# Expert rows of a mixture of experts in 14 blocks instead of 16, with pieces of 32, 64 and 128 columns

## The chip, the cores and the metric

The kernel is one program on one NeuronCore of a Trainium2 chip. Its time is the device time of one execution in microseconds (us). All arithmetic is float32. The profile is of one execution, taken by the hardware profiler; engines are TensorE (PE for matmuls, PEld for its weight loads), VectorE (DVE), ScalarE (ACT), GpSimd (POOL) and SyncE (SP, which here only issues DMAs).

## What is computed

Two layers of a hybrid backbone over 640 tokens (128 context, 512 latent) of width 1024. Each layer has attention, a chunked MLP and a gated recurrence, and then a mixture of 16 experts, of which each token uses two. The change concerns the mixture alone:

```python
eidx = top-2 experts of each token, within its best group of four
dest = place of each (token, expert) row, experts padded to blocks
xb = xt[row_tok].reshape(n_blocks, MOE_BLOCK, D)

def expert_block(args):
    xblk, e = args
    a = jax.nn.silu(xblk @ wg[e]) * (xblk @ wu[e])   # 1024 -> 512, twice
    return a @ wd[e]                                  # 512 -> 1024
yb = lax.map(expert_block, (xb, block_e)).reshape(n_rows, D)
y = jax.ops.segment_sum(yb * row_w[:, None], row_tok, num_segments=T)
```

There are 1280 (token, expert) rows in each layer. An expert has three weight matrices (gate, up, down) of 2 MB each, so a layer reads 48 matrices, 100.7 MB.

## The kernel before

The program is written by hand for each engine; nothing is scheduled by a planner. In the expert stage of a layer the experts are sorted by how many rows they got, on the chip. The expert of rank s has a fixed capacity `CAPS[s]` and a fixed first row `BASES[s]`, and rows beyond a capacity go to overflow blocks, which are run in a loop of `OVB` passes that skip when there is nothing to do (in this execution all are skipped). The capacities sum to 2048 rows, 16 blocks of 128 rows (`NBK`). `RUN` lists the blocks in the order in which they run, with the rank of the first and of the last 64 rows of each: 12 blocks belong to one expert, 4 to two.

TensorE does for each block i, in this order: `hidden(i, 0)` (gate), `tokens_in(i + 1)` (8 transposes of the next block's tokens, L843), `hidden(i, 1)` (up), `outputs(i - 1)` (down of the block before, in two halves of 512 columns) and `turn_hidden(i)` (4 transposes, L866). All three products go through `product` (L855): over k (8 for gate and up, 4 for each half of down) it multiplies the block's 128 columns, which stand still in the array, with 512 columns of an expert's weights. In a block of two experts, two matmuls of 64 columns stand in place of one of 128, and write partitions 0 to 63 and 64 to 127 of the same bank. The program has one float32 matmul where the trace has two instructions.

Weights come through 8 slots of 2 MB (`moe_slots`). `moe_matrices` orders the matrices by the block that needs them first: the gates of a block's new experts, then their ups, then their downs. SP loads matrix m into slot m mod 8, once the last block that uses matrix m - 8 has read it (`moe_used`); `LAST` holds that block. GpSimd gathers a block's token rows from DRAM (L1287), VectorE copies the transposed tokens out (L1849), ScalarE applies silu (L1155) and copies the transposed hidden rows (L1163), VectorE and ScalarE copy a half of the output each (L1855, L1146), and ScalarE's queue stores the block to DRAM (L1151). When all blocks are stored, GpSimd gathers each token's two rows (L1311), ScalarE makes diagonal matrices of the routing weights (L1192), and TensorE combines them (L534, L535).

Of the kernel before, what the change touches and what calls it, by code (L numbers as in the profile page):

```python
# [28 lines left out]
P = 128  # L29
# [29 lines left out]
GB = 4  # L59
NE = 16  # L60
DFF = 512
OVB = 8

CAPS = [256, 256, 192, 192] + [128] * 6 + [64] * 6
BASES = [sum(CAPS[:i]) for i in range(NE)]
NBK = sum(CAPS) // P
NB = NBK + OVB

RUN = [(7, (4, 4)), (0, (0, 0)), (1, (0, 0)), (13, (10, 11)), (2, (1, 1)), (3, (1, 1)), (14, (12, 13)), (4, (2, 2)),
       (5, (2, 3)), (6, (3, 3)), (15, (14, 15)), (8, (5, 5)), (9, (6, 6)), (10, (7, 7)), (11, (8, 8)), (12, (9, 9))]
NSLOT = 8

def moe_matrices():

    order, last = [], {}
    for i, (_, who) in enumerate(RUN):  # L80
        new = [s for s in sorted(set(who)) if s not in last]
        order += [(s, j) for j in range(3) for s in new]
        for s in who:
            last[s] = i
    return order, last

MATS, LAST = moe_matrices()
# [29 lines left out]
def nth(l, per, n):  # L118
    return l * per + n
# [12 lines left out]
def build_program(nc, A):  # L132
    with ExitStack() as ctx:
# [6 lines left out]
        def dram(name, shape):  # L140
            return nc.dram_tensor(name, shape, F32, kind="Internal").ap()
# [5 lines left out]
        x_dram = dram("x_dram", [T, D])  # L147
        exp_dram = dram("exp_dram", [NB * P, D])

# [23 lines left out]
        def view(off, n, pattern=None, **kw):  # L173
            v = ar[:, off:off + n]
            return v.rearrange(pattern, **kw) if pattern else v
# [46 lines left out]
        yb = [view(26624 + 1024 * s, 1024) for s in range(2)]  # L222
# [6 lines left out]
        at_row = view(12288, 10 * P, "p (a r) -> p a r", a=10)  # L229
        at_block = view(12288 + 10 * P, 10 * NB, "p (a b) -> p a b", a=10)  # L230

# [21 lines left out]
        def sm(n):  # L253
            o[0] += n
            return small[:, o[0] - n:o[0]]
# [18 lines left out]
        mhalf = sm(20)  # L274
        spare = sm(OVB)
        modc = sm(4 * KD).rearrange("p (m y k) -> p m y k", m=2, y=2)
        posi = ismall[:, 0:10].rearrange("p (t k) -> p t k", t=NT)
        rowi, blki = ismall[:, 50:60], sb("blki", [P, 10], I32)[:]
        rowf, blkf = sm(10), sm(10)
        ids = ismall[:, 10:10 + NB]  # L280
        novi = ismall[:, 36:37]
        bexi = ismall[:, 40:40 + OVB]
        esi = ismall[:, 62:62 + NE]
# [2 lines left out]
        chosen = view(26624, 80)  # L286
        before = view(27584, 96)
        R9 = view(27680, OVB * NE, "p (j e) -> p j e", j=OVB)
        R9s = view(27808, OVB)
        ck, srt, es, cbs = [view(27816 + NE * i, NE) for i in range(4)]  # L290
        capb = view(27880, 2 * NE, "p (m e) -> p m e", m=2)
        above = view(27912, NE * NE, "p (e f) -> p e f", e=NE)
# [42 lines left out]
        xg_in = [sem("xg_in0"), sem("xg_in1")]  # L335
        xT_done, xT_evac = sem("xT_done"), sem("xT_evac")
        gate_done, up_done, sg_ready, a_ready = sem("gate_done"), sem("up_done"), sem("sg_ready"), sem("a_ready")
        aT_done, aT_ready, y_done = sem("aT_done"), sem("aT_ready"), sem("y_done")
        yA_evac, yB_evac = sem("yA_evac"), sem("yB_evac")
        y_stored = [sem("y_stored0"), sem("y_stored1")]  # L340
# [10 lines left out]
        def until(eng, signal, n):  # L351

            eng.wait_ge(signal, n)
            eng.sem_inc(passed[eng.engine], 1)
# [24 lines left out]
        def moe_used(l, m):  # L380

            s_, j = MATS[m]
            return (gate_done, up_done, y_done)[j], (32 if j == 2 else 16) * l + (LAST[s_] + 1) * (2 if j == 2 else 1)

        def s3(v, k=KD):
            return v.rearrange("p (k c) -> p k c", k=k)
# [21 lines left out]
        def _(sp):  # L408
# [5 lines left out]
            for l in range(DEPTH):  # L414
# [50 lines left out]
                for m in range(len(MATS) - 3, len(MATS)):  # L465
                    until(sp, *moe_used(l, m))
                nov = sp.value_load(novi[0:1, :], min_val=0, max_val=OVB)
                with sp.Fori(0, OVB) as j:
# [25 lines left out]
        def _(pe):  # L494
# [19 lines left out]
            for l in range(DEPTH):  # L514
# [103 lines left out]
                for ci, c in enumerate(JOBS):  # L618
# [21 lines left out]
                    for j in range(NL + 1):  # L640
# [11 lines left out]
                        for w in range(NT):  # L652
                            tk = slice(w * P, (w + 1) * P)
                            for h in range(2):
                                r = slice(64 * h, 64 * h + 64)
# [19 lines left out]
                    if dr == 1:  # L675
# [12 lines left out]
                        for w in range(NT):  # L688
                            ent = (0 if w == 0 else 1 + w, 1 if w == 0 else 2 + w)
                            for d_ in range(2):  # L690
                                for h in range(2):
                                    r = slice(64 * h, 64 * h + 64)
# [114 lines left out]
                for t in range(NT):  # L807
                    pe.wait_ge(tr_evac, nth(l, N_TR, 2 * NT + 2 * t + 2))
                    for half in range(2):
# [3 lines left out]
                        w = s3(slotA(SLOT_OF[7 + half]))  # L813
# [14 lines left out]
                for a in range(2 * NT):  # L828
                    mm = pe.matmul(bank(5)[:, 0:NB], at_row[:, a, :], at_block[:, a, :],
                                   start=a == 0, stop=a == 2 * NT - 1)  # L830
# [3 lines left out]
                def tokens_in(i):  # L834

                    p = i % 2
                    pe.wait_ge(xg_in[p], l * 128 + 16 * (i // 2 + 1))
                    if i:
                        pe.wait_ge(xT_evac, nth(l, NBK, i))
                    if i >= 2:  # L840
                        pe.wait_ge(aT_ready, nth(l, NBK, i - 1))
                    for k in range(KD):
                        mm = pe.transpose(psum[:, 3072 + k * P:3072 + (k + 1) * P], xg[p][:, k * P:(k + 1) * P], ident)  # L843
                    mm.then_inc(xT_done, 1)

                def product(out, act_T, i, j, kn, cs):

                    a, b = RUN[i][1]
                    parts = [(a, slice(0, P))] if a == b else [(a, slice(0, 64)), (b, slice(64, P))]
                    for s_, r in parts:  # L850
                        pe.wait_ge(*moe_landed(l, MAT[s_, j]))
                    for k in range(kn):
                        for s_, r in parts:
                            w = s3(moe_slots[MAT[s_, j] % NSLOT], kn)
                            mm = pe.matmul(out[r, :], act_T[:, k, r], w[:, k, cs], start=k == 0, stop=k == kn - 1)  # L855
                    return mm
# [4 lines left out]
                def turn_hidden(i):  # L861
                    pe.wait_ge(a_ready, nth(l, NBK, i + 1))
                    if i + 1 < NBK:
                        pe.wait_ge(xT_evac, nth(l, NBK, i + 2))
                    for q in range(4):
# [64 lines left out]
        def _(act):  # L930
# [18 lines left out]
            for l in range(DEPTH):  # L949
# [45 lines left out]
                for b, dst, fn in ((1, kf, ACT.Sigmoid), (2, qf, ACT.Copy)):  # L995
# [4 lines left out]
                    for c in (range(5) if b == 1 else (0, 4)):  # L1000
                        pb = unit_ready(AT[b, c])
                        if c < 4:
                            a = act.activation(dst[:, c, P:T], pb, fn)
                        else:
                            a = act.activation(dst[:, :, 0:P], pb.rearrange("p (c t) -> p c t", c=4), fn)
# [20 lines left out]
                for ci, c in enumerate(JOBS):  # L1026
                    at = {second: n for n, first, second in UNITS[ci]}
# [9 lines left out]
                    for j in range(NL):  # L1037
# [4 lines left out]
                        if j == 1:  # L1042
# [4 lines left out]
                            a, b = (kfac, qfac) if c < 2 else (qfac, kfac)  # L1047
# [94 lines left out]
                def y_half(i):  # L1142
                    act.wait_ge(y_done, nth(l, 2 * NBK, 2 * i + 2))
                    if i >= 2:
                        act.wait_ge(y_stored[i % 2], l * 128 + 16 * (i // 2))
                    act.activation(yb[i % 2][:, W:D], bank(5), ACT.Copy).then_inc(yB_evac, 1)  # L1146

                def y_store(i):
                    act.wait_ge(yA_evac, nth(l, NBK, i + 1))
                    act.wait_ge(yB_evac, nth(l, NBK, i + 1))  # L1150
                    act.dma_start(exp_dram[RUN[i][0] * P:(RUN[i][0] + 1) * P, :], yb[i % 2]).then_inc(y_stored[i % 2], 16)  # L1151

                for i in range(NBK):
                    act.wait_ge(gate_done, nth(l, NBK, i + 1))
# [11 lines left out]
                y_half(NBK - 1)  # L1166
                y_store(NBK - 1)

                until(act, y_stored[0], l * 128 + 128)
                until(act, pos_ready, l + 1)  # L1170
                nov = act.value_load(novi[0:1, :], min_val=0, max_val=OVB)
                with act.Fori(0, OVB) as j:
# [17 lines left out]
                for t in range(NT):  # L1190
                    for q in range(2):
                        a = act.activation(by_weight[:, 2 * t + q, :], ident, ACT.Copy, scale=wt[:, t, q:q + 1])  # L1192
# [8 lines left out]
        def _(gp):  # L1201
            gp.memset(condW[:], 0.0).then_inc(cond_zero, 1)
            gp.memset(mhalf, -0.5)
            for s_ in range(NE):
                gp.memset(table[:, 0, s_:s_ + 1], float(CAPS[s_]))
                gp.memset(table[:, 1, s_:s_ + 1], float(BASES[s_]))
            gp.memset(zeros, 0.0)
# [6 lines left out]
            for l in range(DEPTH):  # L1214
# [66 lines left out]
                until(gp, h_stored[0], l * 48 + 48)  # L1281
                until(gp, h_stored[1], l * 32 + 32)
                until(gp, ids_ready, l + 1)
                for i, (blk, _) in enumerate(RUN):
                    if i >= 2:
                        until(gp, xT_done, nth(l, NBK, i - 1))
                    gp.indirect_dma_start(xg[i % 2], None, tok_dram,  # L1287
                                          bass.IndirectOffsetOnAxis(ap=ids[:, blk:blk + 1], axis=0)).then_inc(xg_in[i % 2], 16)
                until(gp, pos_ready, l + 1)
                until(gp, xT_done, nth(l, NBK, NBK))  # L1290
                nov = gp.value_load(novi[0:1, :], min_val=0, max_val=OVB)
# [10 lines left out]
                        gp.dma_start(spare[0:1, bass.ds(j, 1)], bass.AP(A["router_bias"].tensor, 0, [[1, 1], [1, 1]])).then_inc(ov_g, 16)  # L1302
                until(gp, ov_g, l * (16 * OVB) + 16 * OVB)

                until(gp, y_stored[0], l * 128 + 128)
                until(gp, y_stored[1], l * 128 + 128)
                until(gp, ov_st, l * (16 * OVB) + nov * 16 + 16)

                for t in range(NT):
# [15 lines left out]
        def _(v):  # L1325
# [64 lines left out]
            for l in range(DEPTH):  # L1390
# [355 lines left out]
                for t in range(NT):  # L1746
                    dr_()
                    a = tt(before[:, (t + 1) * NE:(t + 2) * NE], before[:, t * NE:(t + 1) * NE], M[:, t, :], ALU.add)
# [52 lines left out]
                for q, oh in enumerate((oh1, oh2)):  # L1801
# [12 lines left out]
                dr_()  # L1814
                tt(at_block, blkf.unsqueeze(2).to_broadcast([P, 2 * NT, NB]),
                   cst[:, C_IOTA:C_IOTA + NB].unsqueeze(1).to_broadcast([P, 2 * NT, NB]), ALU.is_equal)
                tt(at_row, rowf.unsqueeze(2).to_broadcast([P, 2 * NT, P]),
# [33 lines left out]
                def y_half(i):  # L1851
                    v.wait_ge(y_done, nth(l, 2 * NBK, 2 * i + 1))
                    if i >= 2:
                        v.wait_ge(y_stored[i % 2], l * 128 + 16 * (i // 2))
                    v.tensor_copy(yb[i % 2][:, 0:W], bank(4)).then_inc(yA_evac, 1)  # L1855

                tokens_out(0)
# [121 lines left out]
```

## Time and profile before

| | |
|---|---|
| median of 3 runs | 2076.75 us (2075.97 to 2078.27) |
| the profiled execution, its own time | 2085.36 us |
| its span, first to last instruction | 2083.5 us |
| mean granted TensorE clock | 0.936 of 2.4 GHz |
| expert stage, layer 0 / layer 1 | 372.0 / 368.7 us |
| TensorE busy in them | 362.2 / 359.7 us |

The expert stage is taken from the first gate matmul to the end of the last output matmul. In a row of the timeline the first number is the start in us from the span's start and the second the time from the first start to the last end of the instructions that the row merges (xN). Matmuls overlap with the next, so a product's cost is read from its start to the next row's start. What follows in brackets is idle time before the row, and what ended it.

### The profile page before, as it was taken

The page shows a single profiled execution, that of the slowest core. Times are in us where ns is not written, and L with a number is a line of the kernel's source. Part 1 is how long each engine was busy: PE and PEld are TensorE (multiplying, and loading weights), DVE is VectorE, ACT ScalarE, POOL GpSimd, SP SyncE. Part 2 cuts the span into 40 slices and gives each one's busy share as a digit, 9 for nine tenths or more (in the row PEclk, how much of TensorE's full clock was granted, in tenths as well). Part 3 has the DMA queues.
Part 4 walks back from the last instruction along what each step waited for, and adds up shares of the span by engine and source line. Part 5 has one row for each costly group of instructions (what it writes and reads, how often), then busy time and mean ns, then how long its engine had stood idle before and what let it go on. Part 6 is the DMA issues. An engine that isn't in the chain of part 4 may idle for free. (4 is left out here: it accounts for less than half of the span.)

```text
span 2083.5 us, 20602 instructions
## 1 busy us (share of the span) xinstructions
PE 1809.4 (87%) x7528; PEld 927.7 (45%) x7528; DVE 755.3 (36%) x1179; ACT 374.4 (18%) x695; POOL 310.7 (15%) x348
## 2 busy tenths in 40 slices
PE   3999999788956999999799999988798399999983
PEld 1464555554443443434345445554545243443431
DVE  0036567374462110111060575746636310110105
ACT  1323122243010000000141422213411000000002
POOL 0001266000000000000130223630000000000005
PEclk9999999899977999999899999998998599999996
DMA  9421111565019687799603012136121696797934
GB/s 364 151 98 41 36 54 46 207 238 194 21 51 364 251 328 291 286 358 379 220 38 125 13 46 84 47 132 222 54 75 42 249 348 233 294 357 299 393 124 151
DMA packets 142086, 380.43 MB, mean 183 GB/s; under 512 B 9732, under 2 KB 15876, under 8 KB 135332
## 3 DMA queue, kind: packets, MB, share of 16 engines
q1 hardware_dynamic: 111840, 292.31, 37.5%
q10 hardware_dynamic: 21108, 55.36, 7.5%
q0 software_dynamic: 9040, 31.46, 4.1%
q8 instruction: 61, 1.00, 0.2%
q14 instruction: 37, 0.30, 0.0%
HBM read 343.65 MB, written 35.45 MB: 182 GB/s over the span
## 5 line engine op out<-in xcount | busy, mean ns | idle before, releaser
L855 PE MATMUL psum<-sb_arena 128*128 128x512 f32 (+1 forms) x1248 | 494.1, 596 | 10.6 <-DMA sb_arena<-w_up 9.1
L583 PE MATMUL psum<-sb_wA,sb_arena 128*128 128x512 f32 x800 | 365.3, 605 | 0.9 <-DMA sb_wA<-w_in 0.9
L855 PEld LDWEIGHTS psum<-sb_arena 128*128 128x128 f32 (+1 forms) x1248 | 192.5, 171 | 269.7 <-issue 257.7
L855 PE MATMUL psum<-sb_wA,sb_arena 128*128 128x512 f32 (+1 forms) x672 | 278.4, 611 | 9.3 <-DMA sb_wA<-w_up 6.6
L583 PEld LDWEIGHTS psum<-sb_wA,sb_arena 128*128 128x128 f32 x800 | 147.5, 192 | 165.3 <-issue 158.0
L1329 DVE TENSOR_TENSOR sb_arena<-sb_arena 128x320 f32<-128x320 f32 (+8 forms) x252 | 170.8, 719 | 13.4 <-POOL sb_arena L1264 3.8
L1849 DVE COPY sb_arena<-psum 128x1024 f32<-128x1024 f32 x32 | 39.2, 1225 | 344.3 <-PE psum L843 344.3
L855 PEld LDWEIGHTS psum<-sb_wA,sb_arena 128*128 128x128 f32 (+1 forms) x672 | 103.3, 170 | 120.2 <-issue 109.7
L1495 DVE COPY_PREDICATED sb_arena<-sb_masks,psum 128x640 f32<-128x640 uint8 x128 | 112.4, 878 | 90.8 <-PE psum L656 71.5
L574 PE MATMUL psum<-sb_arena,sb_wA 128*128 128x128 f32 (+1 forms) x512 | 140.4, 435 | 0.0
L815 PE MATMUL psum<-sb_wA,sb_arena 128*128 128x512 f32 x320 | 140.3, 599 | 0.0
L1287 POOL DMA_INDIRECT sb_arena<-tok_dram,sb_ismall x32 | 30.3, 946 | 654.1 <-PE psum L843 539.6
L1329 DVE TENSOR_TENSOR sb_arena<-sb_arena,psum 128x512 f32<-128x512 f32 x38 | 26.1, 687 | 272.3 <-PE psum L855 227.7
L1264 POOL TENSOR_TENSOR sb_arena<-sb_arena 128x640 f32<-128x640 f32 x56 | 80.7, 1444 | 287.4 <-ACT sb_arena L1039 251.5
L656 PEld LDWEIGHTS psum<-sb_arena 64*128 64x128 f32 x1280 | 79.4, 193 | 62.8 <-issue 56.1
L656 PE MATMUL psum<-sb_arena 64*128 64x128 f32 x1280 | 91.6, 287 | 14.9 <-DVE sb_arena L1495 12.7
L574 PEld LDWEIGHTS psum<-sb_arena,sb_wA 128*128 128x128 f32 x512 | 77.0, 191 | 60.0 <-issue 59.3
L1146 ACT ACTIVATE sb_arena<-psum 128x512 f32<-128x512 f32 x32 | 19.1, 597 | 461.4 <-PE psum L855 461.4
L1217 POOL TENSOR_TENSOR sb_small<-sb_small 128x4 f32<-128x4 f32 (+3 forms) x24 | 27.5, 1146 | 448.3 <-DVEq L1615 220.1
L815 PEld LDWEIGHTS psum<-sb_wA,sb_arena 128*128 128x128 f32 x320 | 60.9, 192 | 74.8 <-issue 74.8
L1329 DVE TENSOR_TENSOR sb_arena<-psum,sb_gate_mod 128x512 f32<-128x512 f32 (+1 forms) x30 | 26.1, 870 | 133.6 <-PE psum L815 87.8
L1155 ACT ACTIVATE sb_arena<-psum 128x512 f32<-128x512 f32 x32 | 19.2, 599 | 284.2 <-PE psum L855 284.2
(184 smaller groups left out, 1685.1 us busy)
## 6 DMA issues: line engine op xcount, KB each, us to landing
sb_arena<-w_gate SPq DMA_DIRECT2D x22, 2048.0 KB, 18.5
sb_arena<-w_down SPq DMA_DIRECT2D x22, 2048.0 KB, 15.8
sb_wA<-w_up SPq DMA_DIRECT2D x16, 2048.0 KB, 19.4
sb_arena<-w_up SPq DMA_DIRECT2D x16, 2048.0 KB, 15.5
sb_wA<-w_ada SPq DMA_DIRECT2D x13, 2048.0 KB, 7.7
sb_wA<-w_in SPq DMA_DIRECT2D x12, 2048.0 KB, 9.6
sb_arena<-w_ada SPq DMA_DIRECT2D x11, 2048.0 KB, 7.6
sb_wA<-w_gate SPq DMA_DIRECT2D x10, 2048.0 KB, 18.0
```

Of the source, the lines that this page charges most:

```text
L574: mm = pe.matmul(out, w[:, k, cc_ * P:(cc_ + 1) * P], hT[:, k, tok], start=k == 0, stop=k == KD - 1)
L583: mm = pe.matmul(unit_bank(n), hT[:, k, t * P:(t + 1) * P], w[:, k, :], start=k == 0, stop=k == KD - 1)
L656: mm = pe.matmul(U(h)[:, tk], ks[r, tk], qs[r, tk], start=True, stop=True)
L815: mm = pe.matmul(bank(n % 3), hT[:, k, t * P:(t + 1) * P], w[:, k, :], start=k == 0, stop=k == KD - 1)
L855: mm = pe.matmul(out[r, :], act_T[:, k, r], w[:, k, cs], start=k == 0, stop=k == kn - 1)
L1155: act.activation(sg[i % 2], bank(2 * (i % 2)), ACT.Silu).then_inc(sg_ready, 1)
L1217: gp.tensor_tensor(dst, src, mhalf[:, 0:dst.shape[1]], ALU.pow).then_inc(rstd_ready, 1)
L1264: gp.tensor_tensor(Kb[:, j % 2], kf[:, c], Eb[:, (j - 1) % 2], ALU.mult).then_inc(K_ready, 1)
L1287: gp.indirect_dma_start(xg[i % 2], None, tok_dram, bass.IndirectOffsetOnAxis(ap=ids[:, blk:blk + 1], axis=0)).then_inc(xg_in[i % 2], 16)
L1329: return v.tensor_tensor(out, a, b, op)
L1495: v.copy_predicated(w5(ATT[:, dr, h, :]), mk, w5(psum[:, (3 + 2 * h) * 512:(3 + 2 * h) * 512 + T])).then_inc(lv_acc, 1)
L1849: v.tensor_copy(xgT[i % 2], psum[:, 3072:4096].rearrange("p (k t) -> p k t", k=KD)).then_inc(xT_evac, 1)
```

## The change

The capacities are now in steps of 32 rows: 256, 224, 192, 192, 128, four of 96, six of 64, and 32. They sum to 1792, 14 blocks. `ROWS` puts the ranks in a row one behind the other, so that an expert's rows may start in the middle of a block and cross into the next; `block_parts` cuts each block's share into pieces of 128, 64 or 32 rows. Blocks run in the order of their rows. By `block_parts` they are (rank: columns):

| block | pieces | new matrices |
|---|---|---|
| 0 | 8: 64, 8: 32, 15: 32 | 6 |
| 1 | 4: 128 | 3 |
| 2 | 5: 64, 5: 32, 14: 32 | 6 |
| 3 | 14: 32, 6: 32, 6: 64 | 3 |
| 4, 5 | 0: 128 | 3, 0 |
| 6 | 7: 64, 7: 32, 11: 32 | 6 |
| 7 | 11: 32, 1: 32, 1: 64 | 3 |
| 8 | 1: 128 | 0 |
| 9 | 12: 64, 3: 64 | 6 |
| 10 | 3: 128 | 0 |
| 11 | 9: 64, 2: 64 | 6 |
| 12 | 2: 128 | 0 |
| 13 | 10: 64, 13: 64 | 6 |

`OVB` goes from 8 to 10, so that 24 block rows exist as before. The other lines of the diff follow the new count in semaphore values (`PAIR` is the number of even and odd blocks).

```diff
-OVB = 8
+OVB = 10
-CAPS = [256, 256, 192, 192] + [128] * 6 + [64] * 6
-BASES = [sum(CAPS[:i]) for i in range(NE)]
+CAPS = [256, 224, 192, 192, 128] + [96] * 4 + [64] * 6 + [32]
+ROWS = (8, 15, 4, 5, 14, 6, 0, 7, 11, 1, 12, 3, 9, 2, 10, 13)
+BASES = [sum(CAPS[r] for r in ROWS[:ROWS.index(s)]) for s in range(NE)]
 NBK = sum(CAPS) // P
+PAIR = [(NBK + 1) // 2, NBK // 2]
 NB = NBK + OVB
-RUN = [(7, (4, 4)), (0, (0, 0)), (1, (0, 0)), (13, (10, 11)), (2, (1, 1)), (3, (1, 1)), (14, (12, 13)), (4, (2, 2)),
-       (5, (2, 3)), (6, (3, 3)), (15, (14, 15)), (8, (5, 5)), (9, (6, 6)), (10, (7, 7)), (11, (8, 8)), (12, (9, 9))]
+def block_parts(i):
+    parts = []
+    for s in ROWS:
+        at, end = max(BASES[s], i * P) - i * P, min(BASES[s] + CAPS[s], i * P + P) - i * P
+        while at < end:
+            w = next(w for w in (P, 64, 32) if at % w == 0 and at + w <= end)
+            parts.append((s, slice(at, at + w)))
+            at += w
+    return parts
+RUN = [block_parts(i) for i in range(NBK)]
...
                 def product(out, act_T, i, j, kn, cs):
-                    a, b = RUN[i][1]
-                    parts = [(a, slice(0, P))] if a == b else [(a, slice(0, 64)), (b, slice(64, P))]
-                    for s_, r in parts:
+                    for s_ in sorted({s_ for s_, _ in RUN[i]}):
                         pe.wait_ge(*moe_landed(l, MAT[s_, j]))
                     for k in range(kn):
-                        for s_, r in parts:
+                        for s_, r in RUN[i]:
                             w = s3(moe_slots[MAT[s_, j] % NSLOT], kn)
                             mm = pe.matmul(out[r, :], act_T[:, k, r], w[:, k, cs], start=k == 0, stop=k == kn - 1)
...
                 def y_store(i):
-                    act.dma_start(exp_dram[RUN[i][0] * P:(RUN[i][0] + 1) * P, :], yb[i % 2]).then_inc(y_stored[i % 2], 16)
+                    act.dma_start(exp_dram[i * P:(i + 1) * P, :], yb[i % 2]).then_inc(y_stored[i % 2], 16)
...
-                for i, (blk, _) in enumerate(RUN):
+                for i in range(NBK):
                     gp.indirect_dma_start(xg[i % 2], None, tok_dram,
-                                          bass.IndirectOffsetOnAxis(ap=ids[:, blk:blk + 1], axis=0)).then_inc(xg_in[i % 2], 16)
+                                          bass.IndirectOffsetOnAxis(ap=ids[:, i:i + 1], axis=0)).then_inc(xg_in[i % 2], 16)
```

How TensorE's instructions stand, at two places. The first is the start of the expert stage in layer 0. `sb_wA` and `sb_arena` hold the weight slots, `psum` the results; the size is that of the output, columns of the block by 512. Before, block 0: tokens, gate, next tokens, up, hidden transposes, gate of block 1.

```order
L843 MATMUL psum<-sb_cst,sb_arena 128x128 x8
L855 MATMUL psum<-sb_wA,sb_arena 128x512 x8
L843 MATMUL psum<-sb_cst,sb_arena 128x128 x8
L855 MATMUL psum<-sb_wA,sb_arena 128x512 x8
L866 MATMUL psum<-sb_cst,sb_arena 128x128 x4
L855 MATMUL psum<-sb_arena 128x512 x8
```

After, the last two k of block 0's gate (six more like them stand ahead), the next block's tokens, and the first k of its up. In the gate the 64 and the first 32 columns are of rank 8 and the last 32 of rank 15.

```order
L869 MATMUL psum<-sb_wA,sb_arena 64x512
L869 MATMUL psum<-sb_wA,sb_arena 32x512 x2
L869 MATMUL psum<-sb_wA,sb_arena 64x512
L869 MATMUL psum<-sb_wA,sb_arena 32x512 x2
L859 MATMUL psum<-sb_cst,sb_arena 128x128 x8
L869 MATMUL psum<-sb_wA,sb_arena 64x512
L869 MATMUL psum<-sb_wA,sb_arena 32x512
L869 MATMUL psum<-sb_arena 32x512
```

Where one row of 8 whole-width matmuls stood, there are now 24 matmuls in two widths that take turns at each k. The second place is a block of several experts in the middle of the stage, between the hidden transposes and the next tokens. Before, block 3 (64 + 64), where all rows of a product have one width:

```order
L855 MATMUL psum<-sb_arena 128x512 x16
L866 MATMUL psum<-sb_cst,sb_arena 128x128 x4
L855 MATMUL psum<-sb_arena 64x512 x16
L843 MATMUL psum<-sb_cst,sb_arena 128x128 x8
L855 MATMUL psum<-sb_wA,sb_arena 64x512 x16
L855 MATMUL psum<-sb_arena 128x512 x8
```

After, block 3 (32 + 32 + 64): the hidden transposes of block 2 and the first two k of the gate.

```order
L869 MATMUL psum<-sb_wA,sb_arena 128x512 x8
L880 MATMUL psum<-sb_cst,sb_arena 128x128 x4
L869 MATMUL psum<-sb_wA,sb_arena 32x512
L869 MATMUL psum<-sb_arena 32x512
L869 MATMUL psum<-sb_arena 64x512
L869 MATMUL psum<-sb_wA,sb_arena 32x512
L869 MATMUL psum<-sb_arena 32x512
L869 MATMUL psum<-sb_arena 64x512
```

Here too three matmuls stand where one or two stood, and the width changes twice at each k. The blocks of 64 + 64 (9, 11 and 13) have the same rows as before.

## Rows read from the trace of the kernel before

**Rows 1.** The page's first part: busy us, share of the span, instructions.
```profile
PE 1809.4 (87%) x7528; PEld 927.7 (45%) x7528; DVE 755.3 (36%) x1179; ACT 374.4 (18%) x695; POOL 310.7 (15%) x348
```

**Rows 2.** Windows: stretch, us; PE, PEld, DVE, ACT, POOL busy (x); PEclk, DMA share, GB/s.
```profile
650.46:1022.50 372.04, 362.18 (x1144) 157.04 (x1144) 40.44 (x47) 26.86 (x48) 16.81 (x22) 0.98 0.84 312
1657.28:2026.00 368.72, 359.69 (x1144) 156.10 (x1144) 40.45 (x47) 26.85 (x48) 16.82 (x22) 0.99 0.79 298
```

**Rows 3.** Timeline of TensorE: start, us, engine, line, tiles, shape, count; one block.
```profile
669.46 7.03 PE L855 MATMUL psum<-sb_arena 128*128 128x512 f32 x16
676.33 1.04 PE L843 MATMUL psum<-sb_cst,sb_arena 128*128 128x128 f32 x8
...
691.37 7.03 PE L855 MATMUL psum<-sb_arena 128*128 128x512 f32 x16
```

**Rows 4.** Timeline of TensorE, a block of 64 + 64 columns.
```profile
713.38 7.09 PE L855 MATMUL psum<-sb_arena 128*64 128x512 f32 x32
720.40 1.09 PE L843 MATMUL psum<-sb_cst,sb_arena 128*128 128x128 f32 x8
721.42 7.09 PE L855 MATMUL psum<-sb_wA,sb_arena 128*64 128x512 f32 x32
728.44 7.13 PE L855 MATMUL psum<-sb_arena 128*128 128x512 f32 x16
```

**Rows 5.** Timeline of TensorE, single matmuls of a 64 + 64 product.
```profile
752.98 0.64 PE L855 MATMUL psum<-sb_wA,sb_arena 128*64 128x512 f32 x1
752.99 0.64 PE L855 MATMUL psum<-sb_arena 128*64 128x512 f32 x1
753.46 0.59 PE L855 MATMUL psum<-sb_wA,sb_arena 128*64 128x512 f32 x1
...
753.89 0.59 PE L855 MATMUL psum<-sb_wA,sb_arena 128*64 128x512 f32 x1
...
759.48 0.59 PE L855 MATMUL psum<-sb_arena 128*64 128x512 f32 x1
760.00 0.66 PE L866 MATMUL psum<-sb_cst,sb_arena 128*128 128x128 f32 x4
```

**Rows 6.** Timeline of TensorE at the program's start, four pieces of 32 columns.
```profile
38.76 1.89 PE L502 MATMUL psum<-sb_arena,sb_condW 128*32 128x512 f32 x16
```

**Rows 7.** Waits of TensorE in layer 0's stage: total us, times, longest.
```profile
PE psum L855 <- DMA sb_arena<-w_up: 4.5, 2, 2.4
PE psum L855 <- DMA sb_wA<-w_up: 3.7, 1, 3.7
```

**Rows 8.** The same waits in layer 1's stage.
```profile
PE psum L855 <- DMA sb_arena<-w_up: 4.6, 2, 2.4
PE psum L855 <- DMA sb_wA<-w_up: 2.9, 1, 2.9
```

**Rows 9.** Windows over three products that follow a wait.
```profile
815.20:824.00 8.80, 8.76 (x16) 3.53 (x16) 0.00 (x0) 0.00 (x0) 0.00 (x0) 0.81 1.03 401
910.40:920.20 9.80, 9.72 (x18) 4.00 (x20) 0.00 (x0) 0.00 (x0) 0.00 (x0) 0.73 1.03 396
1914.80:1923.70 8.90, 8.85 (x18) 3.64 (x20) 0.00 (x0) 0.00 (x0) 0.00 (x0) 0.81 1.03 400
```

**Rows 10.** SP's waits in layer 0, DMA from 627 to 692, first load's landing, its issue.
```profile
SPq L355 <- PE psum L855: 235.1, 19, 28.3
...
DMA packets 10099, 23.63 MB, mean 363 GB/s; under 512 B 240, under 2 KB 240, under 8 KB 10096
...
sb_wA<-w_gate SPq DMA_DIRECT2D x1, 2048.0 KB, 8.4
...
627.17 0.39 SPq L449 DMA_DIRECT2D sb_wA<-w_gate  x1
```

**Rows 11.** Timeline behind layer 1's stage, ScalarE and TensorE.
```profile
2034.15 3.03 ACT L1192 ACTIVATE sb_arena<-sb_cst,sb_small 128x128 f32<-128x128 f32 x10 [7.58 <-ACTq L1188]
...
2037.00 2.05 PE L534 MATMUL psum<-sb_arena 128*128 128x512 f32 x2 [11.06 <-DMA sb_arena<-exp_dram,sb_ismall]
```

More of the change, by code:

```diff
@@ L79, in moe_matrices @@
     order, last = [], {}
-    for i, (_, who) in enumerate(RUN):
-        new = [s for s in sorted(set(who)) if s not in last]
+    for i, parts in enumerate(RUN):
+        who = sorted({s for s, _ in parts})
+        new = [s for s in who if s not in last]
         order += [(s, j) for j in range(3) for s in new]
@@ L288, in build_program @@
         R9 = view(27680, OVB * NE, "p (j e) -> p j e", j=OVB)
-        R9s = view(27808, OVB)
+        R9s = view(27680 + OVB * NE, OVB)
         ck, srt, es, cbs = [view(27816 + NE * i, NE) for i in range(4)]
@@ L382, in moe_used @@
             s_, j = MATS[m]
-            return (gate_done, up_done, y_done)[j], (32 if j == 2 else 16) * l + (LAST[s_] + 1) * (2 if j == 2 else 1)
+            return (gate_done, up_done, y_done)[j], (l * NBK + LAST[s_] + 1) * (2 if j == 2 else 1)
         def s3(v, k=KD):
@@ L836, in tokens_in @@
                     p = i % 2
-                    pe.wait_ge(xg_in[p], l * 128 + 16 * (i // 2 + 1))
+                    pe.wait_ge(xg_in[p], 16 * (l * PAIR[p] + i // 2 + 1))
                     if i:
@@ L1144, in y_half @@
                     if i >= 2:
-                        act.wait_ge(y_stored[i % 2], l * 128 + 16 * (i // 2))
+                        act.wait_ge(y_stored[i % 2], 16 * (l * PAIR[i % 2] + i // 2))
                     act.activation(yb[i % 2][:, W:D], bank(5), ACT.Copy).then_inc(yB_evac, 1)
@@ L1167, in _ @@
                 y_store(NBK - 1)
-                until(act, y_stored[0], l * 128 + 128)
+                until(act, y_stored[0], 16 * (l + 1) * PAIR[0])
                 until(act, pos_ready, l + 1)
@@ L1303, in _ @@
                 until(gp, ov_g, l * (16 * OVB) + 16 * OVB)
-                until(gp, y_stored[0], l * 128 + 128)
-                until(gp, y_stored[1], l * 128 + 128)
+                until(gp, y_stored[0], 16 * (l + 1) * PAIR[0])
+                until(gp, y_stored[1], 16 * (l + 1) * PAIR[1])
                 until(gp, ov_st, l * (16 * OVB) + nov * 16 + 16)
@@ L1853, in y_half @@
                     if i >= 2:
-                        v.wait_ge(y_stored[i % 2], l * 128 + 16 * (i // 2))
+                        v.wait_ge(y_stored[i % 2], 16 * (l * PAIR[i % 2] + i // 2))
                     v.tensor_copy(yb[i % 2][:, 0:W], bank(4)).then_inc(yA_evac, 1)
```

## Prediction

> **What bounds the kernel now.** I read the page first: TensorE is busy 87% of the span [rows 1], and its costliest group of lines is the expert products (L855), so the question is what TensorE does while the experts run. The windows over the two stages say it [rows 2]: 372.0 us in layer 0 and 368.7 us in layer 1, with TensorE busy 362.2 and 359.7 of them at a granted clock of 0.98 and 0.99. The two stages are 740.7 of 2083.5 us and the diff touches little else. Inside them I read TensorE's timeline for the price of one block, then the waits for weights, then SP's queue, which feeds it.
>
> One whole-width block: gate starts at 669.46, the next block's gate at 691.37, so a block costs 21.91 us [rows 3]. One product in it (8 matmuls in the program, 16 instructions in the trace, each 0.43 us) is 676.33 - 669.46 = 6.87 us. A block of two experts of 64 columns costs nearly the same: 32 instructions from 713.38 to 720.40, 7.02 us, and the next from 721.42 to 728.44, again 7.02 [rows 4]. The reason is in the single rows [rows 5]: the two experts' matmuls start 0.01 us apart, each pair 0.43 us after the last. Four matmuls of 32 columns also share a slot: 16 of them end in 1.89 us, four slots of 0.43 and a tail [rows 6]. So **pieces of one width run side by side**.
>
> The same rows show what a **change of width** costs. Between pairs of one width the step is 0.43 us; the first step after a change is 0.48 (752.98 to 753.46), the last before the next change 0.52 (759.48 to 760.00) [rows 5]. That is 0.05 + 0.09 = 0.14 us a change, and in the program of before there are at most a few in a block: in and out of a product.
>
> **The change, part by part.**
>
> Fewer blocks. 16 blocks become 14 in each layer: 4 x 21.91 = -87.6 us, all of it on TensorE, which waits for nothing else in the stage but a few weights. Blocks of 64 + 64 go from eight to six, each some 0.7 us dearer than a whole one (0.15 a product and the transposes around them): -1.4.
>
> Pieces of mixed width. Five of the 14 blocks in each layer (blocks 0, 2, 3, 6, 7) hold 64 + 32 + 32 columns, and `product` loops over the pieces inside the loop over k. The program's order shows it: 64, 32, 32, 64, 32, 32. So the width now changes twice at each of the 8 k of a product (for the output, twice at each of 4 k in two halves), 16 times a product, where before it changed twice. What no row of before shows is whether a 64-column matmul and a 32-column one, on columns that do not overlap, run side by side. In all rows the matmuls that start together are of one width, and every change of width seen has a step that is longer, not shorter, than 0.43. The bounds are these.
> - Side by side, free changes: a product stays 6.9 us, +0.
> - Side by side, but each change costs its 0.14: 16 x 0.14 = +2.2 a product.
> - One after the other: at each k a group of one width (two instructions) runs 0.48 + 0.52 = 1.00 us and then the other group 1.00. A product is 16 x 1.00 = 16.0 us, +9.1. With only the 0.09 of a change it would be 16 x 0.95 = 15.2 (+8.3); if a group had to end whole (0.59 us, the duration in [rows 5]) before the next starts, 16 x 1.07 = 17.1 (+10.3).
>
> I take one after the other, 16.0 us, because each change in the trace makes TensorE's next group later, which is how an engine looks that empties itself before it changes. By that the product would stay near 6.9 us, which is the first rival below.
>
> There are 3 mixed products a block, 10 mixed blocks in both layers: 30 x 9.1 = +273.9 with the unrounded 9.13. The transposes next to them (L843, L866) see one more change each side: +2.
>
> Waits for weights. Before, TensorE waited 4.5 + 3.7 us in layer 0 [rows 7] and 4.6 + 2.9 in layer 1 [rows 8]. Three of these waits are followed by a product at a reduced clock (granted 0.81, 0.73 in the stretch, so part of it at the lower level of 1.2 GHz): 8.8, 9.6 and 8.8 us instead of 7.0 [rows 9], where the last two rows hold the next product's first pair too, 6.2 us in all. The weights are the same 48 matrices a layer on SP's queue. SP itself waits 235.1 us in the stage for TensorE to free a slot, and while it streams, 363 GB/s bring a matrix of 2.1 MB every 5.8 us [rows 10]. A serial mixed product takes 9 us more, and there are nine of them in the first four blocks, where the demand is highest (18 matrices in the first four blocks). So the waits and their slow products go: -15.7 - 6.2 = -21.9. If the cover is gone they come back, see the rival.
>
> More overflow passes. `OVB` 8 to 10 adds two skipped passes on each engine. On ScalarE, in layer 1, the 8 passes fit in the 7.58 us before L1192, at most 0.95 us each; TensorE starts the combination only at 2037.00, when gathered rows land [rows 11]. Two passes more (1.9 us) bring L1192 to 2036.1 and its first two instructions (0.3 us each) to 2036.7, still ahead. POOL's passes, with a tiny transfer each, are over before the last products. 0, at most +1.9 a layer. Worked out from the reference with its own inputs, the routing fills no rank beyond its new capacity (largest counts 207, 198, 101 and 234, 180, 177, 169 against 256, 224, 192, 192), so no overflow block runs. Descriptor work on ACT and POOL falls with the blocks, and hides behind TensorE.
>
> **Sum**, against the profiled execution's own 2085.4 us: -87.6 - 1.4 + 273.9 + 2 - 21.9 = +165.0, so 2250.4. That execution lies 8.6 us over the median of 2076.75, and the difference is a difference of stages that do not depend on it: 2076.75 + 165 = **2242 us**, 8% slower. With 15.2 and 17.1 us a product, 30 x -0.8 and 30 x +1.1: 2218 to 2275; with what I can't see of the clock, 2215 to 2290.
>
> **The rivals.**
>
> *Mixed widths run side by side* (the other side: faster). For it: disjoint columns, and pairs and quads do so [rows 5, 6]. Against: every change of width costs. The point from which it decides is the mixed product: under 8.3 us (6.9 + 43.8/30) the change gains. Then TensorE needs the gate of block 3, the 16th matrix, at 691.37 + 21.91 = 713.3, and it lands no sooner than 627.17 + 8.4 + 15 x 5.8 = 722 [rows 3, 10], 728 at 6.2 us a matrix when stores and gathers share the engines. That is 9 to 15 us of waits before block 3, and some 2 at block 7, whose weights wait for the slot of block 5's output; before it was 8.2. With two or three slow products after them a layer gains 43.8 less 2 to 12: 32 to 42 us. Both layers: -74, **2003 us** (1993 to 2013).
>
> *Changes cost only their 0.14*: 30 x 2.2 = +66 against -89, waits about as before: **2055 us** (2040 to 2070).
>
> *The drain is worse or the clock falls.* With half the columns at work the granted clock might drop to 1.2 GHz in the mixed products; a product of 16 us would become 32: +480 us, **2720**. Against it: the lower clock came only after idle time [rows 9]. A longer drain ends in the same direction above 2290.
>
> *That it doesn't do what it says*: an overflow block would cost a block and three loads that nothing hides; the counts exclude it.
>
> **How the numbers follow.** One after the other: 0.72, and it holds 2215 to 2290 nine times in ten. Side by side: 0.15. Changes cost only themselves: 0.08. Worse than 2290: 0.05. The likeliest gives 2242. Its own range holds only 0.65, and the nearest case, 2055, only 0.08, so the range must reach the side-by-side case too: 1995 to 2290, about 0.85. Faster by over 0.2% (4 us, about what a measurement of this kernel can tell from no change) 0.20, within 0.2% 0.02 (a mixed product of exactly 8.3 us), slower 0.78.
>
> **What would show it.** In TensorE's timeline of the changed kernel a gate product of block 0, 2 or 3 should last about 16 us, its 64-column rows and its 32-column rows starting a microsecond apart in turn, the two 32-column ones together; the stage should be some 450 us in each layer, with no wait for weights over 1 us and SP waiting longer than before. If instead three rows start within 0.02 us of each other, the product is 7 us and waits of 2 to 5 us for w_gate and w_up appear before block 3, the first rival is right. A step of 0.57 us with all three together is the second.

## The result and the profile after

The changed kernel takes **2248 us** (median of four runs, 2242.1 to 2306.2) against 2077.5 for the kernel before on the same chip (2076.0 to 2080.2): a ratio of **1.081**, 95% interval 1.079 to 1.083, 8% slower. The forecast was 2242. The run of 2306.2 was a disturbed one and is not in the ratio; the other three have a median of 2247.5.

The profiled execution has 2242.1 us of its own. Its page, first part:

```profile
PE 1973.4 (88%) x8152; PEld 873.8 (39%) x8152; DVE 745.9 (33%) x1167; ACT 368.2 (16%) x683; POOL 308.5 (14%) x348
```

TensorE is 164 us busier than in [rows 1]. The windows over the two expert stages, cut as in [rows 2] from the first product to the last:

```profile
645.88:1094.07 448.19, 446.66 (x1456) 131.03 (x1456) 35.24 (x41) 23.73 (x41) 15.98 (x22) 0.99 0.67 245
1734.77:2182.95 448.18, 446.65 (x1456) 131.03 (x1456) 35.24 (x41) 23.72 (x41) 15.97 (x22) 0.99 0.66 241
```

The stages take 448.2 us each where they took 372.0 and 368.7: 155.6 of the 156.7 us by which the two profiled executions differ. The granted clock is 0.99, no lower than before, and the DMA engines are less busy (0.67, 0.66 against 0.84, 0.79). TensorE does not starve; it is slow at its own work. Its timeline shows how, on the up product of block 0 (64 + 32 + 32 columns). A row merges neighbouring matmuls of one pair of tiles, so the `x3` rows hold the two instructions of the 64-column piece and the first one of the 32-column piece from `sb_wA`, which starts with the single one from `sb_arena` in the row below:

```profile
664.67 1.09 PE L859 MATMUL psum<-sb_cst,sb_arena 128*128 128x128 f32 x8
665.69 1.62 PE L869 MATMUL psum<-sb_wA,sb_arena 128*64 128x512 f32 x3
666.70 0.62 PE L869 MATMUL psum<-sb_arena 128*32 128x512 f32 x1
667.15 0.59 PE L869 MATMUL psum<-sb_wA,sb_arena 128*32 128x512 f32 x1
667.15 0.59 PE L869 MATMUL psum<-sb_arena 128*32 128x512 f32 x1
667.68 1.62 PE L869 MATMUL psum<-sb_wA,sb_arena 128*64 128x512 f32 x3
668.69 0.62 PE L869 MATMUL psum<-sb_arena 128*32 128x512 f32 x1
...
681.05 0.59 PE L869 MATMUL psum<-sb_arena 128*32 128x512 f32 x1
```

At 665.69 the 64-column piece starts, alone. The two 32-column pieces start 1.01 us later (666.70), together; their second instructions follow together at 667.15; and at 667.68, 0.98 us after the first pair, the 64-column piece of the next k. One k takes 1.99 us, a product 8 x 1.99 = 15.9 us. So pieces of one width run side by side, and the two widths take turns.

The waits of TensorE in layer 0's stage, and of SP in the same stretch:

```profile
PE psum L869 <- DVE sb_arena L1863: 1.3, 1, 1.3
PE psum L880 <- DVE sb_arena L1343: 0.8, 1, 0.8
PE psum L869 <- ACT sb_arena L1177: 0.7, 1, 0.7
```

```profile
SPq L371 <- PE psum L869: 358.3, 20, 42.6
```

No wait for a weight is left where [rows 7] had 8.2 us, and SP waits 358 us for slots where it waited 235 [rows 10]: both as forecast. What the forecast did not have stands behind layer 0's stage: the combination's first matmul waits 19.0 us, where before it waited 11.4.

```profile
PE psum L550 <- DMA sb_arena<-exp_dram,sb_ismall: 19.0, 1, 19.0
```

Before, the last of it was not a transfer but ScalarE:

```profile
PE psum L534 <- ACT sb_arena L1192: 11.4, 1, 11.4
```

### The profile page after: what moved, and what is told of

The parts are those of the page before. It is cut to its first block and busy times, and to the rows that moved or that the text cites. A ratio compares the mean times of both kernels' runs of the same rounds, so it can differ in the third digit from the quotient of the medians.

```text
span 2240.3 us, 21918 instructions
## 1 busy us (share of the span) xinstructions
PE 1973.4 (88%) x8152; PEld 873.8 (39%) x8152; DVE 745.9 (33%) x1167; ACT 368.2 (16%) x683; POOL 308.5 (14%) x348
## 5 line engine op out<-in xcount | busy, mean ns | idle before, releaser
L869 PE MATMUL psum<-sb_arena 128*32 128x512 f32 (+2 forms) x1600 | 604.2, 602 | 1.5 <-ACT sb_arena L1177 1.5
L869 PE MATMUL psum<-sb_wA,sb_arena 128*32 128x512 f32 (+2 forms) x992 | 405.5, 612 | 2.6 <-DVE sb_arena L1863 2.6
L869 PEld LDWEIGHTS psum<-sb_arena 128*32 128x32 f32 (+2 forms) x1600 | 156.3, 139 | 354.3 <-issue 352.3
L869 PEld LDWEIGHTS psum<-sb_wA,sb_arena 128*32 128x32 f32 (+2 forms) x992 | 94.0, 135 | 242.6 <-issue 239.2
L1863 DVE COPY sb_arena<-psum 128x1024 f32<-128x1024 f32 x28 | 34.3, 1225 | 435.2 <-PE psum L859 435.2
L1160 ACT ACTIVATE sb_arena<-psum 128x512 f32<-128x512 f32 x28 | 16.7, 597 | 540.1 <-PE psum L869 540.1
L1169 ACT ACTIVATE sb_arena<-psum 128x512 f32<-128x512 f32 x28 | 16.8, 599 | 348.3 <-PE psum L869 348.3
```

What stands on the lines that cost most here:

```text
L1863: v.tensor_copy(xgT[i % 2], psum[:, 3072:4096].rearrange("p (k t) -> p k t", k=KD)).then_inc(xT_evac, 1)
```

## The experiments

The theory is that TensorE runs pieces of different width one after the other, each width's turn at one k taking about 1 us. The main rivals are that the number of pieces or experts in a product is what costs, or the change of width alone.

### All pieces of a mixed block 32 wide

```diff
             at += w
+    if any(r.stop - r.start == 32 for _, r in parts):
+        parts = [(s, slice(c, c + 32)) for s, r in parts for c in range(r.start, r.stop, 32)]
     return parts
```

> The changed kernel, but a block that holds a piece of 32 columns is cut wholly into pieces of 32, so no product mixes widths; the blocks, capacities, rows and weights stay. Theory (TensorE runs pieces of different width one after the other): a product of such a block falls from about 15.9 us to about 7.0, 30 of them give back 267 us, and some waits for weights come back before blocks 2 and 3 (10 to 20 us in both layers): about 2003 us, 1993 to 2015, 3 to 4% under the kernel before. Rival (what costs is the number of pieces or of experts in a product, four instructions at each k where two whole ones of 64 stood): the product stays at 16 us or gets dearer, 2248 us or more.

Measured: 2022.9 us against 2082.4 before on that chip, ratio 0.970 (0.968 to 0.973). It has more instructions than the changed kernel (3072 of the products instead of 2592), and takes 10% less time. Its TensorE timeline over the gate product and the start of the up product of block 2:

```profile
697.65 0.66 PE L882 MATMUL psum<-sb_cst,sb_arena 128*128 128x128 f32 x4
698.24 7.07 PE L871 MATMUL psum<-sb_wA,sb_arena 128*32 128x512 f32 x64
705.24 1.09 PE L861 MATMUL psum<-sb_cst,sb_arena 128*128 128x128 f32 x8
708.57 7.91 PE L871 MATMUL psum<-sb_arena 128*32 128x512 f32 x56 [2.24 <-DMA sb_arena<-w_up]
```

The product from 698.24 to 705.24 is block 2's gate: the same rows as in 64 + 32 + 32, in 7.00 us instead of 15.9. The rival (pieces or experts cost) falls: this product has one piece more and the same experts. The stages, and the waits for weights of layer 0:

```profile
648.64:981.93 333.29, 318.94 (x1696) 123.28 (x1696) 35.23 (x41) 23.61 (x41) 16.04 (x22) 0.98 0.88 330
1628.41:1962.13 333.72, 318.93 (x1696) 123.33 (x1696) 35.23 (x41) 23.61 (x41) 16.04 (x22) 0.98 0.86 324
```

```profile
PE psum L871 <- DMA sb_arena<-w_gate: 6.3, 1, 6.3
PE psum L871 <- DMA sb_arena<-w_up: 4.6, 2, 2.3
```

Against [rows 2] the stages gain 38.8 and 35.0 us, inside the 32 to 42 a layer that the prediction gave for this case, and waits for w_gate and w_up are there as it named them, though the longest is 6.3 us where it had 2 to 5. But by its ratio the kernel lies 13 us above the 2003 expected, just outside 1993 to 2015: 0.970 of 2077.5 is 2016. Over half of that is the longer wait behind layer 0's stage, which is here too (18.9 us). From the end of layer 0's stage to the start of layer 1's the traces have 634.8 us before, 640.7 in the changed kernel and 646.5 here; what goes beyond the 7.5 us of the wait was not divided.

### Width outside the loop over k

```diff
-                    for k in range(kn):
-                        for s_, r in RUN[i]:
+                    for width in sorted({r.stop - r.start for _, r in RUN[i]}, reverse=True):
+                        for k in range(kn):
+                            for s_, r in RUN[i]:
+                                if r.stop - r.start == width:
...
```

> The changed kernel, but in a product the loop over widths stands outside the loop over k: all k of the 64-column piece, then all k of the two 32-column pieces. The width changes twice a product instead of 16 times. Theory (one after the other): the two groups still do not overlap, 2 x 16 steps of 0.43 plus 0.3 is about 14.0 us a product, 1.9 less than 15.9, so 30 x -1.9 = -57: 2191 us, 2180 to 2205. Rival (only the change of width costs, and pieces run side by side whatever their width): 16 changes less 2 leaves a product near 7.1 us and the kernel near 2000 to 2015 us.

Measured: 2199.3 us, ratio 1.055 (1.053 to 1.057), which is 2192 on the scale of 2077.5, where 2191 was expected; the changed kernel's ratio was 1.081. The gate product of a mixed block in its timeline, which merges the tail of the one piece into the first row as above:

```profile
711.91 0.66 PE L882 MATMUL psum<-sb_cst,sb_arena 128*128 128x128 f32 x4
712.50 14.07 PE L871 MATMUL psum<-sb_wA,sb_arena 128*64 128x512 f32 x48
726.50 1.09 PE L859 MATMUL psum<-sb_cst,sb_arena 128*128 128x128 f32 x8
```

14.00 us from 712.50 to 726.50. With two changes instead of 16 the product loses 1.9 us, 0.13 for each change, and keeps the other 7.1, of which 0.3 is for the two changes left: the turns are still one after the other. If only changes cost, the product would have taken 7.1. This divides the extra 9.0 us of a mixed product over the 6.9 of a whole-width one: **6.9 because the widths do not overlap, 2.1 for the 16 changes of width**.

### The kernel before, cut 64 + 32 + 32

```diff
-                    parts = [(a, slice(0, P))] if a == b else [(a, slice(0, 64)), (b, slice(64, P))]
+                    parts = [(a, slice(0, P))] if a == b else [(a, slice(0, 64)), (b, slice(64, 96)), (b, slice(96, P))]
```

> The kernel before with its 16 blocks, order and weights, but its four two-expert blocks a layer cut 64 + 32 + 32 instead of 64 + 64. Nothing else moves. Theory: 2 x 4 x 3 = 24 mixed products of 15.9 instead of 7.0 us, +213, less up to 15 us of waits for weights that go: 2275 to 2295 us. Rival (the cost in the changed kernel comes from its order, its gathers or its neighbouring experts, not from the widths): within 1% of 2077.

Measured: 2301.6 us against 2082.4, ratio 1.105 (1.102 to 1.107), from two runs. One line of the kernel before costs 219 us. In its timeline:

```profile
713.61 15.95 PE L855 MATMUL psum<-sb_arena 128*64 128x512 f32 x48
729.49 1.09 PE L843 MATMUL psum<-sb_cst,sb_arena 128*128 128x128 f32 x8
```

15.88 us a product where [rows 4] had 7.02: the same price as in the changed kernel, with none of its blocks, order or gathers. The rival falls. 24 x 8.86 = 213 us. The time came out above my 2275 to 2295, or at its upper end by the ratio (1.105 of 2077.5 is 2295), since I had taken off waits for weights that did not go. In layer 0:

```profile
PE psum L855 <- DMA sb_arena<-w_up: 5.2, 2, 2.8
PE psum L855 <- DMA sb_wA<-w_up: 2.2, 1, 2.2
```

7.4 us where [rows 7] had 8.2. The first of these waits shows why. It is in the block behind the mixed one, and the load that it waits for is issued only when that block has begun. Before, the load and the product that waits for it:

```profile
736.37 0.37 SPq L449 DMA_DIRECT2D sb_arena<-w_up  x1
745.92 7.13 PE L855 MATMUL psum<-sb_arena 128*128 128x512 f32 x16 [2.16 <-DMA sb_arena<-w_up]
```

Then in this kernel:

```profile
754.33 0.37 SPq L449 DMA_DIRECT2D sb_arena<-w_up  x1
764.05 7.13 PE L855 MATMUL psum<-sb_arena 128*128 128x512 f32 x16 [2.34 <-DMA sb_arena<-w_up]
```

The slow products put off the load and its need alike, by 18 us; from the one to the other it is 9.6 us before and 9.7 here. A slower product gives cover only to the loads that run while it does.

### The kernel before, cut 4 x 32

```diff
-                    parts = [(a, slice(0, P))] if a == b else [(a, slice(0, 64)), (b, slice(64, P))]
+                    parts = [(a, slice(0, P))] if a == b else [(s_, slice(c, c + 32)) for s_, c in ((a, 0), (a, 32), (b, 64), (b, 96))]
```

> The kernel before, but its four two-expert blocks a layer cut into four pieces of 32 columns. Theory (pieces of one width run side by side, however many): a product stays at about 7.0 us, the kernel at 2077 us, within 4 us. Rival (each further piece costs): twice the instructions of 64 + 64 in 24 products; at 16 steps of 0.57 a product (each step a change's worth longer) +2.2 each, +54: about 2130; if the pieces ran in pairs, about +165.

Measured: ratio 1.000 (0.999 to 1.002), as expected. Four pieces in 64 instructions take what two take in 32:

```profile
710.95 7.07 PE L855 MATMUL psum<-sb_arena 128*32 128x512 f32 x64
717.95 1.09 PE L843 MATMUL psum<-sb_cst,sb_arena 128*128 128x128 f32 x8
```

### Behind layer 0's stage: w_in after the last store

The wait of 19 us stood in the changed kernel and in both variants of its plan. SP's timeline in the changed kernel, behind its last expert matrix, and the last store on ScalarE's queue:

```profile
1085.90 1.00 SPq L439 DMA_DIRECT2D sb_wA<-w_in  x2
1087.02 5.51 SPq L436 DMA_DIRECT2D sb_wA<-w_in  x1
1092.58 6.88 SPq L437 DMA_DIRECT2D sb_wA<-w_in  x1
```

```profile
1094.80 0.35 ACTq L1165 DMA_DIRECT2D exp_dram<-sb_arena  x1
```

The next layer's w_in loads (6.3 MB, not the 8.4 of the expectation below) start 9 us ahead of the last store, because the slots that they need are freed late, the first of them by the output of block 12. In the kernel before, the last of them is issued at 994.22 and has landed at 1011.4, the last store comes at 1023.14. The experiment below keeps w_in back. It, the one with w_in split and the one on overflow passes start from the all-32 kernel, which was therefore run again:

> The all-32 kernel once more, as the base that the next two are compared with on the same chip. 0.970 of the kernel before, as measured first.

Measured: 0.972 (0.970 to 0.974).

```diff
                 if l + 1 < DEPTH:
+                    until(sp, y_stored[0], 16 * (l + 1) * PAIR[0])
+                    until(sp, y_stored[1], 16 * (l + 1) * PAIR[1])
                     for b in (1, 2, 0):
```

> The all-32 kernel, but SP issues the next layer's w_in loads of layer 0 only when the last outputs are stored. In the all-32 kernel these loads (8.4 MB) are issued at 973.8 us, 9 us ahead of the last store, which then takes 7.6 us to land instead of 2.6, and the first gather 7.3 instead of 4.4; TensorE waits 18.9 us for the gathered rows instead of 11.1. Theory (the store and the gathers share the DMA engines with w_in): the store lands in 2.6 us, TensorE's wait falls by about 5 us (the gathers still meet w_in), 2 to 8 us in all, 0.1 to 0.4% under the all-32 kernel. Rival (the transfers are slow for another reason, such as the block's order or ten overflow passes): the wait stays at 18.9 us; w_in then lands up to 12 us later than it did and the kernel is the same or slower.

Measured: 0.972 (0.970 to 0.975), the same, where 0.1 to 0.4% less was expected. The last store among the DMA issues (KB, us from issue to landing), first in the changed kernel, with w_in under way:

```profile
exp_dram<-sb_arena ACTq DMA_DIRECT2D x1, 512.0 KB, 7.6
```

Then in this kernel, where it is issued at 987.68 and w_in is not yet under way (its first load is issued at 990.47):

```profile
exp_dram<-sb_arena ACTq DMA_DIRECT2D x1, 512.0 KB, 2.6
```

And TensorE's waits behind the stage in this kernel:

```profile
PE psum L554 <- DMA sb_arena<-exp_dram,sb_ismall: 14.3, 1, 14.3
...
PE psum L603 <- DMA sb_wA<-w_in: 4.2, 1, 4.2
```

The store is back to 2.6 us, TensorE's wait falls by 4.7 us, and a new wait of 4.2 us for w_in takes its place. The product behind that wait runs at a granted clock of 0.71 in its window, so partly at the lower level, and takes 9.7 us instead of 6.9:

```profile
1025.66:1035.38 9.72, 9.72 (x16) 4.24 (x17) 0.78 (x4) 0.00 (x0) 0.54 (x1) 0.71 0.01 2
```

So the theory holds for the mechanism and the gain was handed back one step later. The first gather lands in 7.8 us here, 7.3 in the all-32 kernel and 4.4 in the kernel before. In both of the slow cases w_in loads run beside it; that they are the reason was not tested apart.

### Only two of the three w_in matrices after the last store

```diff
                     for b in (1, 2, 0):
+                        if b == 2:
+                            until(sp, y_stored[0], 16 * (l + 1) * PAIR[0])
+                            until(sp, y_stored[1], 16 * (l + 1) * PAIR[1])
```

> The all-32 kernel, but of the next layer's three w_in matrices behind layer 0's stage the first is loaded as soon as its slot is free, as it was, and the other two only when the last outputs are stored. Theory (the last store and the gathers share the DMA engines with w_in): with a third of the bytes ahead of the store TensorE's wait for gathered rows falls from 19.0 to about 15 us, and the first w_in is there in time, so that the wait of 4.2 us for w_in and the slow product behind it, which took the gain back when all three waited, do not come: 3 to 5 us, 0.15 to 0.25% under the all-32 kernel, about 0.969 to 0.971 of the kernel before. Rival (the wait for w_in only moves to the second matrix): no gain.

Measured: 2018.4 us against 2080.3, ratio 0.971 (0.969 to 0.973). The trace does what was expected:

```profile
PE psum L555 <- DMA sb_arena<-exp_dram,sb_ismall: 14.4, 1, 14.4
...
PE psum L604 <- DMA sb_wA<-w_in: 0.2, 1, 0.2
```

4.6 us less before the combination and no wait for w_in. From the end of layer 0's stage to the start of layer 1's its trace has 639.2 us, against 646.5 and 646.0 in the two traces of the all-32 kernel. In time it can't be told from that kernel: its interval overlaps both of that kernel's (0.970 and 0.972). Its profiled execution is the shortest of all (span 2013.3 us); it is some 3% under the kernel before, and whether it beats the all-32 kernel stays open.

### Eight overflow passes instead of ten

```diff
-OVB = 10
+OVB = 8
```

> The all-32 kernel with 8 overflow passes instead of 10. Theory (two skipped passes hide on every engine): the same within 0.1%. Rival (the two passes stand between the last store and the gathers): up to 1.9 us a layer, 4 us or 0.2% faster.

Measured: ratio 0.970 (0.968 to 0.972), all-32 kernel 0.972 (0.970 to 0.974). The intervals overlap, so the times establish no gain and do not exclude the rival's 0.2%. The trace shows none at the places it could be: TensorE's waits before the combination are 19.3 and 11.0 us, as with ten passes (19.0 and 11.3).

## Why the prediction was right, and where it was off

**Fewer blocks, -87.6, and whether mixed widths overlap, +273.9.** The step that decided was the choice between three bounds for a mixed product: 6.9, 9.1 or 16.0 us. It measured 15.9. The first row of evidence I leaned on, that every change of width makes the next start later, did point the right way, but it only priced the change (0.14 forecast, 0.13 measured); that the widths exclude each other, which is 6.9 of the 9.0 us, was an inference that no row of before could carry. The experiments with the width outside the loop and with all pieces at 32 carry it now. The trace agrees with the drain rule of the Trainium skill (TensorEngine Tiling (Array Packing), Key Properties) and not with the reading that distinct columns are enough: they were enough in [rows 5, 6] because the widths were equal. With the measured price the term is 30 x 9.0 = +270.

**Waits for weights, -15.7, and their slow products, -6.2.** The waits went as forecast (no row for a weight in the stage). Of the why I was less right: the kernel before with 64 + 32 + 32 keeps them at 7.4 us a layer although its products are as slow. My reading is that mixed products help only where they stand in the blocks with the high demand, as they do in the changed kernel (blocks 0, 2 and 3); no run moves them apart from the rest.

**The stage as a whole.** Forecast some 450 us a layer, measured 448.2. Both stages together grew by 155.6 us against a forecast of 165: 4 of the 9 are the product at 15.9 instead of 16.0. The rest I did not divide further; the transposes beside mixed products and the slow products behind waits are the terms that I had priced most loosely.

**What was missed: +7.6 us behind layer 0's stage.** The prediction looked behind layer 1's stage [rows 11] for the overflow passes and took layer 0's to be the same. It is not: only layer 0 is followed by w_in loads. The new order frees their slots later, from block 12's output on, so they meet the last store and the gathers. I had counted the moved instructions on TensorE and POOL, and not what SP issues after its last expert matrix. In a kernel whose stage is 76 us longer this hides in the sum, and the profiled executions differ by 156.7 us where the medians (2247.5 and 2077.5) differ by 170.0. The stages grew by 9 us less than forecast. Outside them nothing had been forecast, and there the profiled executions differ by 1 us and the medians by 14, if the stages differ alike in them; 7.6 us of it is the wait. So the nearness of 2242 to 2248 is partly luck: parts that nothing touches (from the program's start to layer 0's stage) took 650.5, 645.9 and 648.6 us in three traces.

**Overflow passes, 0 to +1.9 a layer.** No effect seen in the trace, none that the times establish.

**The rivals.** Side by side (2003 us) would have needed equal widths, and the all-32 kernel is that case: 73.8 us gained in the stages where the rival had 74, 7.5 us lost behind layer 0's stage that it had not. Changes only (2055) is ruled out by the 14.0 us product. The break-even that I gave with the first rival, a mixed product of 8.3 us, was worked out wrongly: 43.8 us is what the dropped blocks gain in one layer, and the 30 mixed products are those of both. By 87.6 us over 30 products it lies near 9.8 us, which also fits my own second rival, faster than before at 9.1 us a product. Nothing in the sum rests on it. The clock did not fall: 0.99 in both stages, though TensorE used half its columns at a time.

## What to carry to other kernels

Before pieces of the array are mixed, find out in the trace whether the sizes run together: here equal widths ran side by side and unequal ones took turns, so cutting all of a mixed block to its smallest piece (64 instructions a product where there were 48, at no cost) turned an 8% loss into a 3% gain. When an order of work changes, follow also the last slots it frees: what is loaded into them next may meet the stores and gathers at the stage's end. And a cover that hides a wait must stand where the wait is, not only be long enough.

## What the runs showed of the hardware

- Two 32-column matmuls and a 64-column one on disjoint columns, moving 512 columns each in 2 instructions: 1.01 + 0.98 us in turns. Four of 32 columns, or two of 64, share steps of 0.43 us, 16 steps in 7.0 us. I had given the turns a chance of 0.72.
- A change of width costs 0.13 us (15.9 - 14.0 over 14 changes); the 14.0 us left is two times 6.87 and two changes.
- Twice the matmul instructions in the same product (64 in 7.00 us, 32 in 7.02) cost nothing measurable.
- A store of 512 KB landed in 2.6 us with no w_in load under way and in 7.6 us with them. I had not expected the last store of a stage to meet them.
